# Shared keys and values of a two-block network: chunks of three stages in one mixed order, values transposed one projection later, weight halves as one operand

## What is computed

```python
def compress_blocks(kv, pos_emb, w1, w2):
...
    flat = blocks.transpose(0, 1, 3, 2, 4).reshape(B, n_cmp, G, CMP_BLOCK * D)
    return jax.nn.gelu(flat @ w1) @ w2

def shared_kv(h, norm_g, w_kv, cmp_pos_k, cmp_w1_k, cmp_w2_k, cmp_pos_v, cmp_w1_v, cmp_w2_v):
    kv = (rmsnorm_2(h, norm_g) @ w_kv).reshape(B, S, N_KV_STREAMS, N_KV_GROUPS, HEAD_DIM)
    k_c, v_c, k_s, v_s, k_w, v_w = [kv[:, :, i] for i in range(N_KV_STREAMS)]
    k_cmp = compress_blocks(k_c, cmp_pos_k, cmp_w1_k, cmp_w2_k)
    v_cmp = compress_blocks(v_c, cmp_pos_v, cmp_w1_v, cmp_w2_v)
    return (k_cmp, v_cmp, partial_rope(k_s), v_s, partial_rope(k_w), v_w)

def nsa_layer(x, kvs, norm_g, w_in, w_out):
    h = rmsnorm_2(x, norm_g)
    proj = h @ w_in
    q = ...
    gates = jax.nn.sigmoid(...)
    z = proj[..., ATTN_D + N_HEADS * N_BRANCH:]
    o = nsa_attention(q, partial_rope(q), gates, *kvs)
    return x + (o.reshape(B, S, ATTN_D) * jax.nn.silu(z)) @ w_out
```

## Time and profile before

| what | us |
|---|---|
| median of 3 runs | 2339.26 (2336.74 to 2346.7) |
| profiled execution, time | 2337.14 |
| its span | 2335.4 |
| PE busy | 2198.3 (94%) |
| DVE busy | 1288.5 (55%) |
| ACT busy | 878.1 (38%) |
| POOL busy | 195.0 (8%) |

### The profile page before, as it was taken

How to read it: one execution, slowest core, us unless ns; L and a number is a source line. 1 busy time by engine, 2 the same in 40 slices (tenths; PEclk the granted TensorE clock), 3 DMA queues, 4 the chain that set the end, 5 groups by cost and what they waited for, 6 DMA issues and landing times.

```text
span 2335.4 us, 32258 instructions
## 1 busy us (share of the span) xinstructions
PE 2198.3 (94%) x10738; PEld 1795.5 (77%) x10738; DVE 1288.5 (55%) x2288; ACT 878.1 (38%) x1645; POOL 195.0 (8%) x110
## 2 busy tenths in 40 slices
PE   7986999999999899999999999999999977999997
PEld 6675777888888778788888888888888766777776
DVE  5876444666643556456666335555554464356663
ACT  4433443332222256533232332222222333555551
POOL 0042220100001111120000121000001100000002
PEclk9997999999999999999999999999999988999998
DMA  3121121233233211133333332333332232200002
GB/s 136 52 84 55 61 63 55 90 99 99 90 99 108 90 37 36 37 99 91 97 94 103 100 108 91 99 96 94 98 99 90 90 105 67 81 19 19 19 10 72
DMA packets 50045, 182.88 MB, mean 78 GB/s; under 512 B 5552, under 2 KB 5680, under 8 KB 49840
## 3 DMA queue, kind: packets, MB, share of 16 engines
q1 hardware_dynamic: 49824, 181.35, 24.3%
q0 software_dynamic: 144, 0.52, 0.1%
HBM read 179.76 MB, written 2.10 MB: 78 GB/s over the span
## 4 chain that ended last, share of the span: by engine, by line
PE 85%; DVE 8%; issue 3%; ACT 3%; DMA 1%; POOL 1%; DVEq 0%; ACTq 0%; POOLq 0%; SPq 0%
PE pj L1971 70%; PE po L2257 3%; PE po L2156 2%; PE ps L2217 2%; PE ps L2110 2%; PE pt L2232 2%; ACT w_hi L668 1%; DMA raw<-in_wstream 1%; PE pt L2126 1%; DVE rtmp L1297 1%; PE pj L2081 1%; PE ps L2349 1%; DVE w_lo L1167 1%; PE po L2165 1%; POOL w_lo L612 0%
## 5 line engine op out<-in xcount | busy, mean ns | idle before, releaser
L1971 PE MATMUL pj<-h_hi,w_hi 128*128 128x512 f32 x1736 | 703.9, 405 | 20.9 <-DVE w_lo L1167 16.1
L1971 PE MATMUL pj<-h_hi,w_lo 128*128 128x512 f32 x1736 | 681.2, 392 | 0.0
L1971 PE MATMUL pj<-h_lo,w_hi 128*128 128x512 f32 x1736 | 681.1, 392 | 0.0
L668 ACT ACTIVATE w_hi<-raw 128x1024 fp32r<-128x1024 f32 x334 | 353.7, 1059 | 856.7 <-PE pj L1971 839.4
L1167 DVE TENSOR_TENSOR w_lo<-raw,w_hi 128x1024 fp32r<-128x1024 f32 x296 | 400.1, 1352 | 390.9 <-ACT w_hi L668 390.7
L1971 PEld LDWEIGHTS pj<-h_hi,w_hi 128*128 128x128 f32 x1736 | 330.1, 190 | 87.7 <-issue 16.9
L1971 PEld LDWEIGHTS pj<-h_hi,w_lo 128*128 128x128 f32 x1736 | 328.8, 189 | 70.4
L1971 PEld LDWEIGHTS pj<-h_lo,w_hi 128*128 128x128 f32 x1736 | 330.1, 190 | 64.7 <-issue 1.4
L1971 PE MATMUL pj<-G_hi,w_hi 128*128 128x512 f32 x704 | 277.3, 394 | 3.1 <-DVE G_lo L1394 3.0
L1971 PE MATMUL pj<-G_lo,w_hi 128*128 128x512 f32 x704 | 275.5, 391 | 0.0
L1971 PE MATMUL pj<-G_hi,w_lo 128*128 128x512 f32 x704 | 275.4, 391 | 0.0
(11 more groups left out here) (323 smaller groups left out, 2595.7 us busy)
## 6 DMA issues: line engine op xcount, KB each, us to landing
raw<-in_wstream SPq DMA_DIRECT2D x334, 512.0 KB, 3.5
xT<-in_x SPq DMA_DIRECT2D x4, 512.0 KB, 9.1
out_x<-xT SPq DMA_DIRECT2D x4, 512.0 KB, 2.7
memT<-in_mem SPq DMA_DIRECT2D x1, 1024.0 KB, 12.0
cst<-in_cst SPq DMA_DIRECT2D x1, 512.0 KB, 10.2
tab<-in_tab POOLq DMA_DIRECT2D x1, 512.0 KB, 5.1
posi<-in_pos SPq DMA_DIRECT2D x1, 256.0 KB, 2.9
vec<-in_vec SPq DMA_DIRECT2D x1, 182.5 KB, 2.5
```

Of the source, the lines that this page charges most:

```text
L668: nc.scalar.activation(w_hi[:, c.par * CW:(c.par + 1) * CW], raw[:, c.par * CW:(c.par + 1) * CW], ACT.Copy).then_inc(hi_ready, 1)
L1971: mm = nc.tensor.matmul(acc, w[:, col:col + P], x[part], start=first and k == 0, stop=last and k == 2)
```

## The change

The chunks of `cmp`, `nkv_s`, `cmp2`, `nkv_w`, `gates` and `nz` become one stage, `shared`, of the same 26 chunks in a mixed order, which each engine's program walks through by name: `ks`, `kw` are key tiles, `vs`, `vw` value tiles, `c0` to `c3` the compression of the keys, `c4` to `c7` that of the values.

```diff
+SHARED = ["ks0", "vs0", "ks1", "c0", "vs1", "c1", "kw0", "c2", "vw0", "c3", "kw1", "c4", "vw1", "c5", "c6", "c7", "gates",
+          "nz0", "nz1", "cmp2", "nz2", "nz3", "nz4", "nz5", "nz6", "nz7"]
-    w_hi, w_lo = put("w_hi", 2 * CW, f32r), put("w_lo", 2 * CW, f32r)
+    w_both = put("w_both", 4 * CW, f32r)
+    w_hi, w_lo = w_both[:, 0:2 * CW], w_both[:, 2 * CW:4 * CW]
+    k_in, k_rot, k_tmp = put("k_in", S, at=mem1), put("k_rot", S, at=mem1 + 2 * KB), put("k_tmp", S, at=mem1 + 4 * KB)
+    v_in = put("v_in", S, at=g0 + 26 * KB)
-        HIDDEN = [po[0], ps[0]]
+        HIDDEN, COMPRESSED = [po[0], ps[0]], [ps[1], po[1]]
```

ACT now copies the rotated keys, and each task stands at a chunk's name (a part of its list):

```diff
+            def spread_keys(branch, pair):
+
+                act.wait_ge(k_roped, (2 if branch == "win" else 0) + pair + 1)
+                for g in range(2):
+                    for hh in range(2):
+                        col = (2 * pair + g) * S
+                        last = nc.scalar.activation(n_k[branch][hh * 64:hh * 64 + 64, col:col + S],
+                                                    k_tmp[g * 64:g * 64 + 64, :], ACT.Copy)
+                last.then_inc(roped, 1)
...
+            for name in SHARED:
+                c, t = shared_at(name)
+                split_hi(c + 2)
+                if name == "ks0":
+                    window_hi(1)
+                if name == "vs0":
+                    spread_keys("slc", 0)
...
+                if name == "kw1":
+                    hidden_tanh(0)
+                if name == "c4":
+                    turned_values("win", 0)
+                if name == "vw1":
+                    spread_keys("win", 1)
+                if name == "c5":
+                    hidden_hi(0)
```

DVE (also in part); the two halves of a compression's bank are added here, and the gelu's end is a task of its own:

```diff
+            def hidden_in(which):
+
+                c = shared_at(("c3", "c7")[which])[0]
+                bank_ = COMPRESSED[which]
                 complete(c)
+                link(nc.vector.tensor_copy(hidx[:, :], bank_[:, 0:2 * P]))
+                link(nc.vector.tensor_tensor(hidx[:, :], hidx[:, :], bank_[:, 2 * P:4 * P], ALU.add))
...
+            for k in range(4):
+                split_lo(At(CH["cmp_kv"] + k + 2))
+                take_kv(k)
+                if k >= 2:
+                    dve.wait_ge(folded, 2)
+                    window(k - 2)
...
+            for name in SHARED:
+                c, t = shared_at(name)
+                split_lo(c + 2)
...
+                if name in ("c3", "c7"):
+                    hidden_in(("c3", "c7").index(name))
+                if name in ("c4", "gates"):
+                    hidden_out(("c4", "gates").index(name))
```

PE: one matmul takes both weight halves as a moving operand of 2 x 256 columns into the two halves of a whole bank, and a value is transposed behind a later chunk than its own:

```diff
-                        for k, (x, w) in enumerate(((win_hi, w_hi), (win_hi, w_lo), (win_lo, w_hi))):
-                            mm = nc.tensor.matmul(pj[t.par][:, 0:2 * P], x[which][:, here], w[:, cols],
-                                                  start=l == 0 and k == 0, stop=l == 15 and k == 2)
+                    both = w_both[:, :].rearrange("p (a c) -> p a c", a=2)[:, :, at:at + 2 * P]
+                    nc.tensor.matmul(bank_[:, :].rearrange("p (a c) -> p a c", a=2), win_hi[which][:, here], both,
+                                     start=l == 0, stop=False)
+                    mm = nc.tensor.matmul(bank_[:, 0:2 * P], win_lo[which][:, here], w_hi[:, at:at + 2 * P],
+                                          start=False, stop=l == 15)
...
+            turned_behind = {"ks1": ("vs0", TN["nv_s"]), "kw0": ("vs1", TN["nv_s"] + 1), "kw1": ("vw0", TN["nv_w"]),
+                             "c6": ("vw1", TN["nv_w"] + 1), "nz0": ("gates", TN["gates"])}
+            for name in SHARED:
+                c, t = shared_at(name)
+                if name[:-1] == "c":
+                    compressed(name)
+                elif name == "cmp2":
+                    compressed_out(c)
+                else:
+                    project(c, t, h_hi, h_lo, norm="q2" if name == "gates" else None)
+                if name in turned_behind:
+                    of, number = turned_behind[name]
+                    turn(shared_at(of)[1], number, src=v_in[:, :])
+                if name == "c4":
+                    turn_hidden(0)
+                if name == "nz0":
+                    turn_hidden(1)
+                if name == "nz2":
+                    turn(At(SHARED_TILE["cmp2"] + 1), TN["cmpv"], src=v_in[:, :])
```

More of the change, by code:

```diff
@@ new lines, in value_tile @@
+            def value_tile(c, t, number):
+                complete(c)
+                dve.wait_ge(v_turned, number)
+                scaled("kv2", v_in[:, :], t)
+            for k in range(4):
[4 more added lines that the diff above has]
+                    window(k - 2)
+            dve.wait_ge(ld["tab2"], 16)
+            for name in SHARED:
+                c, t = shared_at(name)
+                split_lo(c + 2)
+                if name in ("ks0", "ks1", "kw0", "kw1"):
+                    key_tile(c, t, ("ks0", "ks1", "kw0", "kw1").index(name))
+                if name in ("vs0", "vs1", "vw0", "vw1", "gates"):
+                    value_tile(c, t, TN["nv_s"] + ("vs0", "vs1", "vw0", "vw1", "gates").index(name))
+                if name == "ks0":
+                    window_lo(0)
+                if name == "vs0":
+                    window_lo(1)
+                    dve.wait_ge(folded, 4)
+                    window(2)
+                if name == "ks1":
+                    window(3)
+                if name == "vs1":
+                    window_lo(2)
+                if name == "c1":
+                    window_lo(3)
+                if name in ("c3", "c7"):
+                    hidden_in(("c3", "c7").index(name))
+                if name in ("c4", "gates"):
+                    hidden_out(("c4", "gates").index(name))
+                if name == "c6":
+                    hidden_lo(0)
+                    for m in range(DT):
+                        lowest("q2", m, m % 2)
+                if name == "nz1":
+                    hidden_lo(1)
+                if name == "cmp2":
@@ L2475, in _, with compressed_out @@
-            kv_tiles("nkv_w", "nv_w")
-            project(At(CH["gates"]), At(TL["gates"]), h_hi, h_lo, norm="q2")
-            turn(At(TL["gates"]), TN["gates"])
-            with pe.Fori(0, 4) as i:
-                for k in range(2):
-                    project(At(CH["nz"] + k, i, 2), At(TL["nz"] + k, i, 2), h_hi, h_lo)
+            def compressed_out(c):
+                arrived(c)
+                for which in range(2):
+                    t = At(SHARED_TILE["cmp2"] + which)
+                    free(t)
+                    pe.wait_ge(hid_ready, which + 1)
+                    for m in range(2):
+                        here = slice((2 * which + m) * P, (2 * which + m + 1) * P)
+                        mm = product(pj[t.par][:, 0:P], 2 * which + m, c.par, (hid_hi[:, here], hid_lo[:, here]), m == 0, m == 1)
+                mm.then_inc(chunk_used, 1)
```

272 lines of the change are left out of this document (114 added, 158 removed).

## The result

The changed kernel takes 2322.31 us (median of 5 runs, 2314.09 to 2323.84), the kernel before, run beside it on the same chip, 2346.7 (5 runs, 2336.74 to 2347.39; three of them are those that the forecast started from, with a median of 2339.26). The ratio is 0.991, with a 95% interval of 0.988 to 0.9939: faster by 0.9%. The forecast was 2323 in a range of 2311 to 2334, with 0.74 on faster by over 0.5%; it was right.

A forecast was written before the change was run, and what follows sets the result against it. The touched stretch was taken as bound by what feeds PE: work 111.8, waits 26.1 and low clock 4.7 make 142.6 us against 158.5, 15.9 less. That gives 2321.2, plus 2.1 for the median: 2323 us, range 2311 to 2334.

The forecast's parts named there:

- the forecast's stretch: From the last `cmp_kv` projection's end to the last `nz` projection's end: 158.5 us before, 142.6 forecast.
- hidden transposes: PE waits behind c4 for DVE's hidden unit, issued after a key tile and c5's split: 6.0 us.
- rest above 111.8: Low clock on top of 111.8 us of PE work in the stretch: 4.7 us.
- Low clock: Half clock loses 2.0 us after the hidden transposes, 2.0 in nz2 and 0.7 in `cmp2`: 4.7 us.
- rival 3: Waits of about 1 us keep the clock at 1.2 GHz from vs1 to nz1: 2358 us, chance 0.04.
- Weight halves: Compression steps with one doubled operand, two matmuls for three: 1.43 us per chunk, no gain.
- Key copies on ACT: Moves 1.73 us per key tile off DVE, puts 2.6 on ACT, hidden except in c7's 1.7 wait.
- Values transposed later: Value transposes one projection later: three waits of up to 3.5 us go, only 0.4 is left.
- Rival 4: The stretch's waits only change names and their sum stays: 2339 us, chance 0.04.
- Rival 1: Small waits shrink by 5 us, hidden transposes by 3, low clock by 2: 2313 us, chance 0.17.
- rival 2: Three more clock dips (6 us) and a third on the small waits (3 us): 2332 us, chance 0.2.
- three signs of being wrong: Wait behind c4 under 3 us, clock between c0 and c4 under 0.9, or stretch's PE waits above 32 us.

The follow-up runs named there:

- the first experiment: Changed kernel with the transposes of the keys' hidden unit behind vw1 instead of c4: stretch 155.66 us against 162.21, median 2317.64 us.
- the eighth experiment: Changed kernel with later hidden transposes, `cmp2` in its own banks and the values' windows behind later chunks: stretch 144.77 us, median 2310.56 us.
- the ninth experiment: Changed kernel with the keys' compression chunks c0 to c3 in a row ahead of kw1: stretch 165.79 us against 162.21, median 2326.72 us.

## Why the prediction was right

By its own steps, with the waits of PE in the forecast's stretch (from 1863.22 to 2003.34 in the changed kernel):

| term | forecast | measured |
|---|---|---|
| ks1; vs0's transposes | 1.1; 0.4 | 0.79; none |
| vs1, c1, kw0 | 2.2, 1.2, 1.3 | 2.04, 0.88, 0.98 |
| vw0, kw1 | 0.7, 1.2 | 0.62, 1.07 |
| hidden transposes | 6.0 | 6.03 |
| c6, c7 | 1.2, 1.7 | 1.43, 1.34 |
| gates | 2.6 | 1.94 |
| `cmp2`, nz2 | 3.8, 2.7 | 3.56, 2.76 |
| sum of waits | 26.1 | 23.4 |
| rest above 111.8 | 4.7 | 4.8 (116.60 − 111.8) |
| stretch to the last `nz` | 142.6 | 140.1 |
| its end | about 2006 | 2003.3 |

- **The mixed order.** Each wait came where it was forecast, but for the 0.4 at vs0's transposes, and each within 0.7 us. The sum was 2.7 too high: all but one of the small waits by 0.1 to 0.4, the gates by 0.7. Two came in part through others than forecast. At ks1 PE waits for the bank that DVE frees by scaling ks0 (`k_in`), behind the split. Ahead of the gates' norm ACT's split of their chunk stood idle 1.20 for the chunk's load; the prediction had named this place ("at most 1 us") but not put it into the sum, so up to 1.2 of the 1.94 are the load's.
- **Hidden transposes behind c4.** 6.03 against 6.0, and the first experiment shows that it was this order and nothing else.
- **Low clock.** Against the eighth experiment, which ran at full clock, it cost 1.6 from kw1 to the gates, where 2.0 were forecast, and 2.1 from nz2 on, for 2.0. The windows of the changed kernel have it where the forecast put it, behind the hidden transposes and behind `cmp2`, and nowhere between vs1 and c4:

```profile
1883.00:1919.00 36.00, 29.88 (x137) 23.60 (x136) 25.74 (x33) 16.89 (x22) 0.00 (x0) 1.00 0.39 122
...
1924.00:1934.00 10.00, 8.99 (x34) 7.18 (x34) 0.77 (x2) 1.51 (x2) 0.00 (x0) 0.79 0.18 55
...
1963.00:1975.00 12.00, 8.51 (x28) 6.93 (x29) 2.11 (x4) 3.62 (x5) 0.00 (x0) 0.60 0.28 89
```

- Of 36 us with five waits of 0.6 to 2.0 none is at the lower level, which is what the earlier trace rows had promised and what rival 3 denied. The Trainium skill, page "TensorE: Matmul & The Clock Gate", section "Loop structure matters more than you think", shows a loop with a long DMA wait between its matmuls and says that PE goes cold in it. That is not the case of these 36 us, whose waits are short, between whole chunks and not for loads. With four of them in a row, in the ninth experiment, the clock behind them was 0.70.
- **Weight halves.** No gain; taken at nothing, measured at 0.03.
- **Table loads.** 1.28 each with no drain, as the sum had it.
- **Key copies on ACT.** Hidden on ACT, as forecast. But the prediction priced only what the edit adds to ACT (in c7's 1.7) and gave no gain to the 1.73 per tile that it takes from DVE's chain; without the edit the stretch is 7.0 us longer.
- **Values transposed later.** Forecast as "in this": right in the total, and the split that it left open is now known. It is not one of several parts of equal rank but the part without which the changed stretch is longer than before.
- **The rest of the kernel.** Forecast as unchanged; the sweep took 3.46 more. Of the gain of 18.41 in the stretch 14.8 is left in the span. Without this the profiled execution would have come 2.3 below the 2321.2 of the forecast, and with it 1.2 above: two errors of opposite sign. That the medians lie 0.7 us from the forecast is luck: it compared with a median of 2339.26, which became 2346.7 with two more runs, and the 24.4 us between the medians are 6 more than the stretch gave.
- **Rivals.** Rival 4 falls with the waits for `vraw`, which are gone. Rival 1 had the direction of the small waits right but wanted 10 us; rival 2's further dips did not come, though one of them, at the gates, did in the first experiment. None of the three signs of being wrong came: the wait behind c4 is 6.03, the clock between c0 and c4 1.00, the waits 23.4.

## What to carry to other kernels

When a result of one engine is consumed by a later instruction of an in-order engine, move the consumer one long piece of work later than feels necessary: here that was worth 24 us for the four value tiles and the gates in the mixed order, 6.5 for the hidden unit, and without it a mix of chunks that balances the queues gained nothing. Count waits one by one along each in-order queue, by rows, also those that the new order creates; they came within 0.7 us each. Look at the loads too where short chunks follow each other. And spread the waits that are left: the same 5.7 us of them cost 1.6 us of low clock right behind them when they lay together, and none when spread.
